# Where a convolution's layer norm and gate stand among the rounds of an attention

## The chip, the core and the metric

The kernel runs on one core of a Trainium2 chip. The metric is the device time of one execution in microseconds. Before the change it was 1478.38 us, the median of three runs (1476.76 to 1479.64).

## The reference

Two layers of a hybrid encoder, for 512 prompt tokens and 64 sample tokens (with a cache of 512). In each layer a normalised and modulated input goes through one projection. Half of its columns feed a sparse attention (8 heads, the best 256 or fewer keys per query). The other half feeds a convolution module, and both halves meet in one output projection:

```
g = a * jax.nn.sigmoid(b)
...
attn = dsa_attention(q, iq, iw, pos, k_all, v_all, ik_all, k_pos)
y = conv(padded) + conv_b                       # depthwise, width 31, 512 channels
y = jax.nn.silu(layer_norm(y, ln_conv_g, ln_conv_b))
mix = jnp.concatenate([attn, y], axis=-1)
x = x + gt_a * (mix @ w_out)
```

with `layer_norm(y) = (y - mean) * rsqrt(var + EPS) * g + b` over the 512 channels. A mixture of 16 experts follows in each layer.

## The kernel before

All tokens lie in five tiles: four of 128 (prompt) and one of 64 (sample). Channels lie on partitions for the convolution: `cy` is 128 x 4 x 576, four blocks of channels by all tokens. There is no planner; each engine has its own program written out by hand, and semaphores (`L["..."]`) tie them together. An engine works its list strictly in order.

The convolution is computed before the attention's softmax part. Its layer norm begins there as well: the mean is taken off `cy` on VectorE (L1461, `lnx`), the squares are made on GpSimd (L1785), summed over channels by TensorE with a matrix of ones (L720, L721), and scaled into `lnb`, the variance of every token, 128 x 576 (L1507, L1508, `lnr` = 1). What is left of it:

- the square root of `lnb` on ScalarE (L1162, `lnr` = 2)
- its reciprocal on VectorE (L1517)
- the product of `cy` with it on VectorE (L1519, `lny`)
- the gate function Silu on ScalarE, with the norm's gain and bias as the activation's scale and bias, one instruction for each of four channel blocks (L1178, `mixy`). It writes `hT[:, 4:8]`, half of the output projection's input.

The attention runs in ten rounds, n = 0 to 9, one for each group of four heads of one tile. The tiles come in the order 0, 4, 3, 2, 1, with 128, 576, 512, 384 and 256 keys. The stages of different groups overlap. In round n:

- TensorE turns group n's probabilities (L500 from L729), computes the logits of group n + 2 (L699, L700), in layer 0 also 16 matmuls of a later modulation in rounds 2 to 9 (L520), and multiplies group n's turned probabilities with V (L747).
- ScalarE copies the output of group n - 1 out (`outputs`, L1140), copies the turned probabilities of group n to SBUF (L1155), scales the probabilities of group n + 1 (`normalised`, L1132), and computes the exponentials of group n + 2 (`exps`, L1121).
- VectorE inverts the sums of group n + 1 (`inverses`, L1501), and adds the mask and takes the maxima of group n + 2 (`masked`, L1477, L1480, L1489).

In round 3 ScalarE's queue also issues the loads of gate vectors and norm vectors (L1168 to L1173), and in layer 0 in rounds 3 and 7 it stores modulation rows (`keep_mod`, L936).

Behind the rounds stands the output projection (`project_out`, L781): for each tile, 8 matmuls of 512 columns for each half of w_out. TensorE starts it once all four gate instructions (`mixy`) and all ten output copies (`on`) are there (L751, L752). The weights come through a ring of six slots; a slot is loaded by SyncE's queue (L378) when TensorE has released it.

ScalarE evaluates Exp, Sqrt and Silu from tables, and the program has an ACT_TABLE_LOAD where it goes from one to another. Copies and scalings have none of their own.

Of the kernel before, what the change touches and what calls it, by code (L numbers as in the profile page):

```python
# [20 lines left out]
ALU = mybir.AluOpType  # L21
ACT = mybir.ActivationFunctionType
AX = mybir.AxisListType

P = 128
# [5 lines left out]
TOK = SEQ + DEC  # L31
# [43 lines left out]
def rows_of(t):  # L75
    return P if t < 4 else DEC
# [23 lines left out]
def program(nc, A, O):  # L100
    ctx = ExitStack()
    with ctx:
        def sb(name, shape, dt=F32):
            return ctx.enter_context(nc.sbuf_tensor(name, shape, dt))

        def sem(name):
            return ctx.enter_context(nc.semaphore(name))
# [8 lines left out]
        hT = sb("hT", [P, KC, TOK])  # L116
# [3 lines left out]
        vT = sb("vT", [P, 52])  # L120
# [21 lines left out]
        def part(at, n, *shape):  # L142
            v = arena[:, at:at + n]
            if len(shape) == 2:
                return v.rearrange("p (a b) -> p a b", a=shape[0])
            if len(shape) == 3:
                return v.rearrange("p (a b c) -> p a b c", a=shape[0], b=shape[1])
            return v
# [8 lines left out]
        cy = part(17336, 2304, 4, TOK)  # L157
# [9 lines left out]
        lnb = part(8704, 576)  # L167
# [60 lines left out]
        L = {n: sem("l_" + n) for n in names}  # L228
# [61 lines left out]
        def chunks_of(t):  # L290

            return [(c, P) for c in range(t + 1 if t < 4 else 4)] + ([(4, DEC)] if t == 4 else [])
# [4 lines left out]
        def logit_bank(job):  # L297

            return job % 3 if job < 8 else job % 2 if job < 16 else (job + 2) % 3
# [605 lines left out]
        def _(act):  # L905
            S = nc.scalar
# [32 lines left out]
            for l in range(DEPTH):  # L939
# [13 lines left out]
                for k in range(0, KC, 2):  # L953
                    act.wait_ge(L["nT"], k + 1)
                    S.activation(hT[:, k, 0:SEQ], ps[k][:, :], ACT.Identity, bias=vT[:, k:k + 1],
                                 scale=small[:, S_AT + k:S_AT + k + 1]).then_inc(L["nTa"], 1)
                act.wait_ge(L["nT"], 9)
                for k in range(0, KC, 2):
                    S.activation(hT[:, k, SEQ:TOK], ps[0][:, k * DEC:(k + 1) * DEC], ACT.Identity, bias=vT[:, 16 + k:17 + k],
                                 scale=small[:, S_AT + 8 + k:S_AT + 9 + k]).then_inc(L["nTa"], 1)  # L960
# [152 lines left out]
                def exps(n):  # L1113
                    t, g = GROUPS[n]
                    m = rows_of(t)
                    act.wait_ge(L["nmx"], n + 1)
                    for i in range(4):
                        r = PR[0:m, 4 * (n % 2) + i, 0:NKEYS[t]]
                        h = S_SUM + 8 * ((n // 2) % 2) + 4 * g + i
                        q = S_NMX + 4 * (n % 2) + i  # L1120
                        ins = S.activation(r, r, ACT.Exp, bias=small[0:m, q:q + 1], accum_out=small[0:m, h:h + 1])  # L1121
                    ins.then_inc(L["pexp"], 1)

                def normalised(n):

                    t, g = GROUPS[n]
                    m = rows_of(t)
                    act.wait_ge(L["inv"], n + 1)
                    for i in range(4):
                        h = S_INV + 4 * (n % 2) + i  # L1130
                        r = PR[0:m, 4 * (n % 2) + i, 0:NKEYS[t]]
                        ins = S.mul(r, r, small[0:m, h:h + 1])  # L1132
                    ins.then_inc(L["pn"], 1)

                def outputs(n):

                    t, g = GROUPS[n]
                    m = rows_of(t)
                    act.wait_ge(L["pv"], n + 1)
                    S.copy(hT[:, g:g + 3:2, t * P:t * P + m],  # L1140
                           ps[6 + n % 2][:, 0:2 * m].rearrange("p (j t) -> p j t", j=2)).then_inc(L["on"], 1)
# [6 lines left out]
                for n, (t, g) in enumerate(GROUPS):  # L1148
                    m = rows_of(t)
                    if n >= 1:  # L1150
                        outputs(n - 1)
                    for q, (c, kn) in enumerate(chunks_of(t)):
                        job = PT0[n] + q
                        act.wait_ge(L["pt"], job + 1)
                        S.copy(pT[0:kn, c, 0:4 * m], ps[4 + job % 2][0:kn, 0:4 * m]).then_inc(L["pta"], 1)  # L1155
                    if n + 1 < len(GROUPS):
                        normalised(n + 1)
                    if n + 2 < len(GROUPS):
                        exps(n + 2)
                    if n == 7:  # L1160
                        act.wait_ge(L["lnr"], 1)
                        S.activation(lnb[:, :], lnb[:, :], ACT.Sqrt).then_inc(L["lnr"], 1)  # L1162
                    if n == 3:
                        act.wait_ge(L["lnr"], 1)
                        if l == 0:
                            act.wait_ge(s_mst, 64)
                            keep_mod(2)
                        act.dma_start(gt[:, 0, :], mrows[0, 2].broadcast_to([P, D])).then_inc(L["gt_ld"], 16)  # L1168
                        act.dma_start(gt[0:DEC, 1, :], mrows[1, 2].broadcast_to([DEC, D])).then_inc(L["gt_ld"], 16)
                        for b, q in enumerate((4, 3)):  # L1170
                            act.dma_start(AB[0][:, b, :], mrows[0, q].broadcast_to([P, D])).then_inc(L["ab_ld"], 16)
                            act.dma_start(AB[1][0:DEC, b, :], mrows[1, q].broadcast_to([DEC, D])).then_inc(L["ab_ld"], 16)
                        act.dma_start(gf[:, :], A["g_norm_ffn"][l:l + 1].broadcast_to([P, D])).then_inc(L["ab_ld"], 16)  # L1173
                    if l == 0 and n == 7:
                        keep_mod(3)
                act.wait_ge(L["lny"], 1)
                for c in range(4):
                    S.activation(hT[:, 4 + c, :], cy[:, c, :], ACT.Silu, bias=vT[:, 48 + c:49 + c],  # L1178
                                 scale=vT[:, 44 + c:45 + c]).then_inc(L["mixy"], 1)
                outputs(9)  # L1180
                if l == 0:
                    keep_mod(4)
# [102 lines left out]
        def _(dve):  # L1285
            V = nc.vector
# [22 lines left out]
            for l in range(DEPTH):  # L1309
                n_chain = [0]  # L1310

                def chain(ins):

                    n_chain[0] += 1
                    ins.then_inc(L["dch"], 1)
                    dve.wait_ge(L["dch"], n_chain[0])
# [147 lines left out]
                def masked(n):  # L1464

                    t, g = GROUPS[n]
                    m = rows_of(t)
                    mk = C[0:m, K_M0:K_M0 + P] if t == 0 else msk[0:m, MSK_AT[t]:MSK_AT[t] + NKEYS[t]]
                    if n >= 2:
                        dve.wait_ge(L["pt"], PT0[n - 2] + len(chunks_of(GROUPS[n - 2][0])))  # L1470
                    for i in range(4):
                        job = 4 * n + i
                        dve.wait_ge(L["lgt"], job + 1)
                        r = PR[0:m, 4 * (n % 2) + i, :]
                        k = min(NKEYS[t], 512)
                        mx = S_MX + i
                        ins = V.tensor_tensor_reduce(r[:, 0:k], ps[logit_bank(job)][0:m, 0:k], mk[:, 0:k], 0.125, MARK, ALU.add, ALU.max,  # L1477
                                                     small[0:m, mx:mx + 1])
                        if t == 4:
                            ins = V.tensor_tensor_reduce(r[:, 512:576], ps[2 + job % 2][0:m, 0:DEC], mk[:, 512:576], 0.125, MARK,  # L1480
                                                         ALU.add, ALU.max, small[0:m, mx + 4:mx + 5])
                        ins.then_inc(L["ttr"], 1)
                    dve.wait_ge(L["ttr"], 4 * n + 4)
                    if t == 4:
                        chain(V.tensor_tensor(small[0:m, S_MX:S_MX + 4], small[0:m, S_MX:S_MX + 4], small[0:m, S_MX + 4:S_MX + 8], ALU.max))
                    if n >= 2:
                        dve.wait_ge(L["pexp"], n - 1)
                    q = S_NMX + 4 * (n % 2)
                    V.tensor_scalar(small[0:m, q:q + 4], small[0:m, S_MX:S_MX + 4], -1.0, None, ALU.mult).then_inc(L["nmx"], 1)  # L1489
                    dve.wait_ge(L["nmx"], n + 1)  # L1490
# [18 lines left out]
                for n in range(len(GROUPS)):  # L1509
                    if n + 1 < len(GROUPS):  # L1510
                        inverses(n + 1)
                    if n + 2 < len(GROUPS):
                        masked(n + 2)
                    if l == 0 and n == 5:
                        add_bias(3, 3)
                dve.wait_ge(L["lnr"], 2)
                chain(V.reciprocal(lnb[:, :], lnb[:, :]))  # L1517
                dve.wait_ge(L["lnx"], 1)
                V.tensor_tensor(cy[:, :, :], cy[:, :, :], lnb[:, :].unsqueeze(1).to_broadcast([P, 4, TOK]), ALU.mult).then_inc(L["lny"], 1)  # L1519


                if l == 0:
# [331 lines left out]
```

## Time and profile before

| | |
|---|---|
| median of 3 runs | 1478.38 us |
| the profiled execution | 1482.77 us |
| its span, first to last instruction | 1480.9 us |
| mean granted TensorE clock | 0.896 |
| TensorE busy | 1252.0 us, 85% |
| VectorE busy | 551.3 us, 37% |
| ScalarE busy | 362.0 us, 24% |
| GpSimd busy | 152.5 us, 10% |

The ten rounds lie at about 334 to 418 us in layer 0 and 1065 to 1150 us in layer 1. Times in the rows are microseconds from the span's start. Idle time of an engine that is not the bottleneck costs nothing, so the table alone says little on a change within the rounds; the chain of waits and the timeline of the rounds do.

### The profile page before, as it was taken

What the parts mean: (1) busy time and instruction counts of PE and PEld (TensorE: products, weight loads), DVE (VectorE), ACT (ScalarE), POOL (GpSimd) and SP (SyncE); (2) the same over time, 40 slices, a digit from 0 to 9 for tenths busy, and PEclk for the clock granted to TensorE, in tenths of its full rate; (3) what the DMA queues carried; (4) which work ended last, traced back from release to release, by engine and by line L of the source; (5) the groups of instructions that cost most, each with busy time, mean ns of one, the idle gap of its engine ahead of it and who ended that gap; (6) DMA issues with size and microseconds to landing.
All of it is one profiled execution on the core that took longest, in us unless ns stands there. A gap on an engine that the chain in (4) does not pass through costs nothing.

```text
span 1480.9 us, 15896 instructions
## 1 busy us (share of the span) xinstructions
PE 1252.0 (85%) x6139; PEld 724.7 (49%) x6139; DVE 551.3 (37%) x1418; ACT 362.0 (24%) x828; POOL 152.5 (10%) x218
## 2 busy tenths in 40 slices
PE   3998799987899779999707998998777996999990
PEld 0552244443545466777504533454445454777770
DVE  1118687023244521111042058980324353311115
ACT  2124110036831111111122133001368111211111
POOL 0401140010001150000021013100100011000002
PEclk7999799987999889999857989899858997999995
DMA  9438996351941589999580120223211016699985
GB/s 363 121 114 318 359 310 184 105 198 57 308 170 56 191 285 346 365 366 368 189 288 4 57 69 29 72 54 105 66 49 30 0 58 234 205 364 370 361 300 210
DMA packets 137173, 284.97 MB, mean 192 GB/s; under 512 B 11613, under 2 KB 91909, under 8 KB 130697
## 3 DMA queue, kind: packets, MB, share of 16 engines
q1 hardware_dynamic: 116416, 209.70, 42.0%
q0 software_dynamic: 8352, 42.50, 8.4%
q10 hardware_dynamic: 12329, 31.74, 6.1%
q8 instruction: 49, 0.80, 0.2%
q14 instruction: 27, 0.22, 0.0%
HBM read 237.91 MB, written 52.40 MB: 196 GB/s over the span
## 4 chain that ended last, share of the span: by engine, by line
PE 70%; DVE 11%; DMA 6%; ACT 6%; issue 4%; SPq 1%; POOL 1%; ACTq 1%; DVEq 0%; POOLq 0%
PE ps L490 46%; PE ps L781 9%; PE ps L500 6%; PE ps L639 3%; PE ps L700 3%; ACT arena L1121 2%; DMA W<-in_w_gate 2%; DMA X<-in_x_sample 2%; DVE arena L1426 1%; SPq L400 1%; DMA arena<-y_d,sid 1%; DVE arena L1477 1%; PE ps L520 1%; PE ps L600 1%; DVE arena L1387 1%
## 5 line engine op out<-in xcount | busy, mean ns | idle before, releaser
L490 PE MATMUL ps<-W,arena 128*128 128x256 f32 (+1 forms) x1280 | 347.0, 427 | 8.5 <-DMA W<-in_w_gate 3.2
L490 PEld LDWEIGHTS ps<-W,arena 128*128 128x128 f32 x1280 | 241.8, 193 | 83.3 <-issue 53.6
L490 PE MATMUL ps<-W,hT 128*128 128x512 f32 (+3 forms) x480 | 190.6, 557 | 7.7 <-DVE gt L1305 7.7
L500 PE MATMUL ps<-C,arena 128*128 128x128 f32 (+3 forms) x851 | 127.3, 295 | 65.3 <-ACT arena L1155 15.7
L500 PEld LDWEIGHTS ps<-C,arena 128*128 128x128 f32 (+3 forms) x851 | 104.1, 157 | 102.3 <-issue 32.1
L781 PE MATMUL ps<-W,hT 128*128 128x512 f32 (+1 forms) x320 | 144.8, 607 | 5.7 <-ACT hT L1178 5.7
L490 PE MATMUL ps<-hT,W 128*128 128x64 f32 (+1 forms) x512 | 142.6, 440 | 7.1 <-ACT arena L1044 7.1
L490 PEld LDWEIGHTS ps<-W,hT 128*128 128x128 f32 (+1 forms) x480 | 86.9, 184 | 110.4 <-issue 87.2
L490 PEld LDWEIGHTS ps<-hT,W 128*128 128x128 f32 x512 | 78.9, 193 | 72.2 <-issue 64.3
L781 PEld LDWEIGHTS ps<-W,hT 128*128 128x128 f32 (+1 forms) x320 | 57.1, 183 | 80.1 <-issue 73.7
L1689 DVE TENSOR_TENSOR arena<-arena,ps 128x256 f32<-128x256 f32 x32 | 13.5, 421 | 215.1 <-ACT arena L1219 215.1
L1386 DVE MAX8 small<-arena 64x8 f32<-64x576 f32 (+3 forms) x132 | 80.5, 610 | 3.7
L1387 DVE MATCH_REPLACE8 arena<-small,arena 64x576 f32<-64x576 f32 (+3 forms) x132 | 78.4, 594 | 0.0
L639 PE MATMUL ps<-arena 128*32 128x64 f32 (+1 forms) x1024 | 66.5, 418 | 5.3 <-DMA arena<-arena 5.3
L1790 POOL DMA_INDIRECT x_d<-arena,sid x30 | 28.8, 960 | 380.1 <-DVE sid L1599 366.8
L520 PE MATMUL ps<-W,scT 128*32 128x512 f32 x384 | 58.3, 706 | 11.1 <-DMA W<-in_w_ada 10.7
L700 PE MATMUL ps<-arena 64*128 64x128 f32 (+4 forms) x160 | 56.2, 623 | 10.9 <-DVE small L1477 10.5
L1818 POOL DMA_INDIRECT arena<-y_d,sid x20 | 20.1, 1004 | 403.7 <-DMA y_d<-arena 200.3
L1219 ACT ACTIVATE arena<-ps 128x256 f32<-128x256 f32 x32 | 12.3, 383 | 190.8 <-PE ps L490 190.8
L1121 ACT ACTIVATE arena<-arena,small 128x128 f32<-128x128 f32 (+4 forms) x80 | 47.3, 592 | 44.4 <-DVE small L1489 44.3
L1684 DVE COPY arena<-ps 128x512 f32<-128x512 f32 x32 | 22.1, 691 | 93.1 <-PE ps L490 93.1
L1477 DVE CUSTOM_DVE_ANT_0 arena<-ps,arena 64x512 f32<-64x512 f32 (+3 forms) x64 | 35.9, 587 | 55.6 <-PE ps L700 55.1
(244 smaller groups left out, 1106.8 us busy)
## 6 DMA issues: line engine op xcount, KB each, us to landing
W<-in_w_ada SPq DMA_DIRECT2D x48, 1024.0 KB, 7.5
W<-in_w_gate SPq DMA_DIRECT2D x32, 1024.0 KB, 10.4
W<-in_w_up SPq DMA_DIRECT2D x32, 1024.0 KB, 12.8
W<-in_w_down SPq DMA_DIRECT2D x32, 1024.0 KB, 7.7
arena<-x_d SPq DMA_DIRECT2D x33, 512.0 KB, 11.1
y_d<-arena ACTq DMA_DIRECT2D x33, 512.0 KB, 7.3
W<-in_w_in SPq DMA_DIRECT2D x16, 1024.0 KB, 7.3
arena<-arena SPq DMA_DIRECT2D x128, 79.2 KB, 2.1
```

The lines of the kernel that those rows point to most:

```text
L490: ins = T.matmul(out, l, r, start=n == 0, stop=n == len(pairs) - 1, skip_group_check=True)
L500: count(T.transpose(o, i, ident[0:m, 0:m]), done if n == len(outs_ins) - 1 else None)
L520: ins = T.matmul(out[32 * j:32 * j + 32, :], scT[:, k, :], W[:, use % 6, 512 * j:512 * j + 512], start=k == 0, stop=k == KC - 1, skip_grou ...
L639: ins = T.matmul(ps[b][32 * g:32 * g + 32, 0:n], W4[:, i % 2, NQ * g + q, :], G4[i % 2][:, g, s0 + 4 * q:s0 + 4 * q + n], start=q == 0, st ...
L700: T.matmul(ps[logit_bank(job)][0:rows_of(t), 0:b - a], q, kT[1][hp, a:b], start=True, stop=True).then_inc(L["lgt"], 1)
L781: ins = T.matmul(ps[5 + n % 3][0:rows_of(t), :], hT[:, 4 * q + k, tokens(t)], wv[:, k, :], start=q == 0 and k == 0, stop=last, skip_group_ ...
L1121: ins = S.activation(r, r, ACT.Exp, bias=small[0:m, q:q + 1], accum_out=small[0:m, h:h + 1])
L1386: chain(V.max(m8, sc))
L1387: chain(V.match_replace(sc, m8, sc, MARK))
L1477: ins = V.tensor_tensor_reduce(r[:, 0:k], ps[logit_bank(job)][0:m, 0:k], mk[:, 0:k], 0.125, MARK, ALU.add, ALU.max, small[0:m, mx:mx + 1])
L1684: V.tensor_copy(ys[:, u, 512:1024], ps[7][:, :]).then_inc(L["yd"], 1)
L1790: G.indirect_dma_start(out=x_d[:, :], out_offset=bass.IndirectOffsetOnAxis(ap=table[0:m, 5 * k + t:5 * k + t + 1], axis=0), in_=HR[0:m, t, ...
```

## The change

The four leftover steps of the layer norm are moved into the rounds; none is added or taken away:

- the square root, on ScalarE, from round 7 to round 0 (behind the exponentials of group 2)
- the reciprocal, on VectorE, from behind round 9 to round 2 (behind the maxima of group 4)
- the product, on VectorE, from behind round 9 to round 3 (behind the maxima of group 5)
- the four gate instructions, on ScalarE, from behind round 9 to round 7 (behind the exponentials of group 9, where the square root was)

```
-                    if n == 7:
+                    if n == 0:
                         act.wait_ge(L["lnr"], 1)
                         S.activation(lnb[:, :], lnb[:, :], ACT.Sqrt).then_inc(L["lnr"], 1)
...
+                    if n == 7:
+                        act.wait_ge(L["lny"], 1)
+                        for c in range(4):
+                            S.activation(hT[:, 4 + c, :], cy[:, c, :], ACT.Silu, bias=vT[:, 48 + c:49 + c],
+                                         scale=vT[:, 44 + c:45 + c]).then_inc(L["mixy"], 1)
                     if l == 0 and n == 7:
                         keep_mod(3)
-                act.wait_ge(L["lny"], 1)
-                for c in range(4):
-                    S.activation(hT[:, 4 + c, :], cy[:, c, :], ACT.Silu, bias=vT[:, 48 + c:49 + c],
-                                 scale=vT[:, 44 + c:45 + c]).then_inc(L["mixy"], 1)
                 outputs(9)
...
                         masked(n + 2)
+                    if n == 2:
+                        dve.wait_ge(L["lnr"], 2)
+                        chain(V.reciprocal(lnb[:, :], lnb[:, :]))
+                    if n == 3:
+                        dve.wait_ge(L["lnx"], 1)
+                        V.tensor_tensor(cy[:, :, :], cy[:, :, :], lnb[:, :].unsqueeze(1).to_broadcast([P, 4, TOK]),
+                                        ALU.mult).then_inc(L["lny"], 1)
                     if l == 0 and n == 5:
                         add_bias(3, 3)
-                dve.wait_ge(L["lnr"], 2)
-                chain(V.reciprocal(lnb[:, :], lnb[:, :]))
-                dve.wait_ge(L["lnx"], 1)
-                V.tensor_tensor(cy[:, :, :], cy[:, :, :], lnb[:, :].unsqueeze(1).to_broadcast([P, 4, TOK]), ALU.mult).then_inc(L["lny"], 1)
```

## Rows read from the trace of the kernel before

**Rows 1.** The page, parts 1 and 4: busy engines, and the chain's shares.

```profile
PE 1252.0 (85%) x6139; PEld 724.7 (49%) x6139; DVE 551.3 (37%) x1418; ACT 362.0 (24%) x828; POOL 152.5 (10%) x218
...
PE 70%; DVE 11%; DMA 6%; ACT 6%; issue 4%; SPq 1%; POOL 1%; ACTq 1%; DVEq 0%; POOLq 0%
```

**Rows 2.** Chain of waits, layer 1's end: start, us, engine and line.

```profile
1137.28 1.28 ACT L1162
...
1145.15 1.28 ACT L1178
...
1146.45 3.15 ACT hT L1178 x4
...
1149.94 15.26 PE ps L781 x31
```

**Rows 3.** Chain of waits, layer 0's end.

```profile
408.56 3.77 DVE arena L1517
...
412.35 2.57 DVE arena L1519
...
414.95 0.87 ACT hT L1178
...
418.44 1.82 PE ps L781 x3
```

**Rows 4.** Timeline, layer 1's end: start, us, engine, line, count [idle before, released by].

```profile
1139.17 0.35 ACT L1140 COPY hT<-ps 128x256 f32<-128x256 f32 x1
...
1144.55 0.58 ACT L1155 COPY arena<-ps 128x512 f32<-128x512 f32 x1 [0.27 <-PE ps L500]
...
1145.28 1.97 PE L747 MATMUL ps<-arena,vrow 128*64 128x128 f32 x16 [0.77 <-ACT arena L1155]
...
1149.49 0.35 ACT L1140 COPY hT<-ps 128x256 f32<-128x256 f32 x1
```

**Rows 5.** Timeline, layer 0's end.

```profile
408.69 1.07 ACT L1155 COPY arena<-ps 128x512 f32<-128x512 f32 x2
...
409.91 1.09 PE L747 MATMUL ps<-arena,vrow 128*64 128x128 f32 x16
...
411.41 1.09 PE L500 MATMUL ps<-C,arena 128*128 128x128 f32 x8 [0.41 <-ACT arena L1132]
...
413.20 1.28 ACT L1178 ACT_TABLE_LOAD   x1
...
414.29 1.09 PE L747 MATMUL ps<-arena,vrow 128*64 128x128 f32 x16
```

**Rows 6.** Timeline, ScalarE in round 1, layer 1 and then layer 0.

```profile
1074.96 2.77 ACT L1132 ACTIVATE arena<-arena,small 64x576 f32<-64x576 f32 x4
...
1079.67 0.78 ACT L1121 ACTIVATE arena<-arena,small 64x576 f32<-64x576 f32 x1 [1.94 <-DVE small L1489]
...
348.87 0.78 ACT L1121 ACTIVATE arena<-arena,small 64x576 f32<-64x576 f32 x1 [1.94 <-DVE small L1489]
```

**Rows 7.** Timeline, layer 1, the small reciprocals of groups 4 and 5 and group 4's scaling.

```profile
1094.56 0.18 DVE L1501 RECIPROCAL small<-small 128x4 f32<-128x4 f32 x1 [3.05 <-ACT arena L1121]
...
1097.03 2.56 ACT L1132 ACTIVATE arena<-arena,small 128x512 f32<-128x512 f32 x4
...
1105.50 0.18 DVE L1501 RECIPROCAL small<-small 128x4 f32<-128x4 f32 x1 [3.05 <-ACT arena L1121]
```

**Rows 8.** Layer 0's end: SyncE's queue, and w_out's issues with time to landing.

```profile
405.62 6.52 SPq L378 DMA_DIRECT2D W<-in_w_out  x4
...
W<-in_w_out SPq DMA_DIRECT2D x4, 1024.0 KB, 7.1
```

**Rows 9.** Windows: us, busy by engine, granted clock (PEclk), DMA share, GB/s.

```profile
418.00:424.00 6.00, 5.56 (x9) 2.41 (x10) 0.00 (x0) 0.34 (x2) 0.00 (x0) 0.72 1.08 358
1137.00:1147.00 10.00, 5.59 (x40) 4.77 (x40) 6.49 (x3) 8.44 (x16) 0.00 (x0) 0.64 0.00 0
1149.00:1155.00 6.00, 5.06 (x8) 2.27 (x9) 0.00 (x0) 0.84 (x2) 0.00 (x0) 0.63 0.01 3
```

## The prediction

> **What bounds the kernel now.** I read the page's shares and its chain first. TensorE is busy for 85% of the span, but that is a mean over stages; the chain gives it 70%, with ScalarE and VectorE taking turns in between [rows 1]. The change touches only the ten attention rounds of each layer, so I read the chain of waits there, and then the timeline around each moved instruction. At the end of layer 1's rounds ScalarE alone carries the chain: table load and square root, copies, table load and the four gate activations, then the output projection at 1149.94 [rows 2]. At the end of layer 0 the chain goes through VectorE: square root, reciprocal 3.77 us, product 2.57 us, gate, projection at 418.44 [rows 3]. So the same code ends differently in the two layers, and each has to be summed for itself. Everything behind the projection hangs on its start, so I let a shift here pass on whole.
>
> **Edit 1, square root from round 7 to round 0.** In round 7 the table load of 1.28 and the square root stand ahead of the next copy: it starts at 1139.17, where without it it could have started at about 1137.18 (the exponentials are done at 1137.27, and a copy starts 0.1 ahead of that end), so 2.0 us [rows 2, 4]. In round 0 the same 2.0 us come behind the exponentials of group 2. Round 7 used no exponential after it; round 0 does, so a load for the exponential is added once per layer, 1.28 us, behind the scaling of group 2 and ahead of the exponentials of group 3. Loads need not wait for the data: the one for the gate in layer 0 ran at 413.20, and the gate then waited for the product that ended at 414.92 [rows 3, 5]. So I place it in the idle time if there is any. There is: the scaling runs from 1074.96 for 2.77 us, and the exponentials of group 3 wait 1.94 us for VectorE's maxima and start at 1079.67; layer 0 has the same 1.94 us [rows 6]. Nothing behind the maxima of group 3 needs what is delayed (its logits and maxima follow from scaled group 1). New start: 1079.73 (scaling done, 2.0 later) + 0.02 + 1.28 + 0.02 = 1081.05, so 1.38 us later than before. From there ScalarE's exponentials, its copies out of PSUM and TensorE's transposes alternate, and I see no second idle time on ScalarE that belongs to an outside event. I take +1.38 us in each layer. Bounds: 0, if a later round absorbs it (idle before exponentials exists in nearly every round, but is itself set by the loop), and 3.27 (2.0 + 1.28), if none of it is covered.
>
> **Edit 2, reciprocal and product into rounds 2 and 3 on VectorE.** Behind the maxima of group 4 VectorE sits idle for 3.05 us up to the small reciprocal of group 4 at 1094.56 [rows 7]. The wide reciprocal needs 3.77 there, so the small one comes 0.7 late, at about 1095.3; its reader, ScalarE's scaling, starts only at 1097.03 [rows 7], so 1.7 us are left: no cost. The product needs 2.57, and the idle time before the small reciprocal of group 5 (1105.50) is 3.05 again: no cost. If the cover were gone, each would cost its excess over 3.05, at most 0.7 us per layer. What it takes off is the chain of 3.77 and 2.57 at the end of layer 0, and nothing in layer 1, where ScalarE is late anyway. GpSimd issues nothing in these rounds, and no DMA is moved past either.
>
> **Edit 3, the gate from behind the rounds into round 7.** Load and four activations take 1.28 + 3.15; from the load to the next copy it is 1149.49 - 1145.15 = 4.34 us [rows 2, 4]. In round 7 it stands in the square root's place, ahead of the copy of group 7's output, the copies of group 8's transposes, its product with V, the transposes and copies of group 9. All of these move by 4.34 - 1.90 (load to copy before, 1139.17 - 1137.28 = 1.89) = +2.45 us, since ScalarE has no idle time there that it could use.
>
> *Layer 1's end.* Before: the last copy ended at 1145.13, TensorE's product of group 9 ran from 1145.28 for 1.97 us to 1147.25, quite hidden under the gate. After: it ends at 1147.25 + 2.45 = 1149.70; then the output copy that it releases (0.04 + 0.37), and 0.10 to the projection: 1150.21 against 1149.94 [rows 2, 4], +0.27 us. The gate leaves the end, and the product behind it comes into view.
>
> *Layer 0's end.* Before, VectorE's chain kept the projection to 418.44. After: transposes of group 9 at 411.41 + 2.45 = 413.86, 16 modulation matmuls behind them and the product of group 9, which began at 414.29, at 416.74; + 1.09 + 0.41 + 0.10 = 418.34 [rows 3, 5]: -0.10 us. The last w_out load waits for a slot that these transposes release: it is issued at 412.14 at the latest now, 414.6 then, and lands 7.1 us later at about 421.7 [rows 8]; it is needed by the thirteenth matmul of the projection, 418.34 + 12 x 0.43 = 423.5 [0.43: 13.3 of the chain's 15.26 us for 31 matmuls at full clock, rows 2]. Hidden, with 1.8 us to spare.
>
> Sum without the clock: layer 0 +1.38 - 0.10 = +1.28, layer 1 +1.38 + 0.27 = +1.65, together +2.93 us.
>
> **TensorE's clock.** In layer 0 it idled 3.06 us under the gate (product done at 415.38, projection at 418.44) and the projection's first 6 us were granted 0.72 of the clock: 6 x 0.28 = 1.7 us lost. In layer 1 the clock was at the low level, 1.2 GHz, already for the last product, and the projection's first 6 us got 0.63 [rows 4, 5, 9]: 2.2 us lost over these, 1.7 of it behind 1149.94. After the change the wait right before the projection is about 0.5 us in both. Against that a new wait of 2.3 us opens in layer 0 (the copies that the product of group 8 needs are over at 408.69 + 1.07 + 2.45 = 412.21, so it moves from 409.91 to 412.25 [rows 5], while the matmuls before it end where they did), and in layer 1 the wait in round 7 grows from 3.7 to 6.1 us with the clock already down behind it. Bounds: 3.4 us back (both projections at 2.4 GHz at once), or as much lost (a later rise in the longer pauses of rounds 1 to 3 in both). I take 0.7 us back, near the lower end, because the pause is moved and not removed.
>
> Forecast: +2.93 - 0.7 = +2.2 us. The profiled execution took 1482.77 us (span 1480.9 and 1.9 around it), so 1485.0 for such a one; it lies 4.4 above the median of the plain runs, 1478.38, so I predict 1480.6.
>
> *A rule that speaks against the change.* The trace shows 1.28 us for a load, with the gate 0.02 behind it [rows 2]. The Trainium skill ("ScalarE: Activation LUTs", "What ACT_TABLE_LOAD costs") adds a drain of about 1.38 us to each change of set. By it round 0's two loads would be 2.76 dearer, and the sum 5.5 us higher, 1486.1. The trace contradicts it: in layer 1's end the last copy is over at 1145.13 and the load begins at 1145.15 [rows 2, 4], so there is no room for a drain, and this rule gets no chance of its own. The page's other rule, all exponentials first and then all square roots, is what the kernel before obeys and this change breaks: by the trace's price that is the 1.28 us per layer of edit 1.
>
> **The rivals.**
> *The clock pays for it (chance 0.2).* The shift of 2.93 stands, but TensorE enters both projections at full clock: 2.93 - 3.4 = -0.5 us, 1477.9. For it: the wait right before them shrinks from 2.7 and 3.1 to 0.5 us. Against: rows 9 show the low clock well before layer 1's projection.
> *The shift is absorbed (0.1).* The reload hides in later rounds' idle time, +1.38 goes to 0 twice, and with the clock's 3.4 it is 0.17 - 3.4 = -3.2 us, 1475.2: faster. For it: ScalarE idles before most exponentials. Against: each such idle time is ended by VectorE's maxima, which follow from ScalarE's own earlier copies.
> *The pauses cost the clock more (0.2).* The longer pause in round 1 and the one in round 7 keep the clock low for longer, in each layer by as much as the pause before the projection costs now, 1.7: +2.93 + 2 x 1.7 = +6.3 us, 1484.7, slower. It decides if the rounds' matmuls behind the pause run at 1.2 GHz where they ran at 2.4 before. For it: layer 1's rounds 1 to 3 already run low. Against: the clock is low there anyway, so there is little to lose.
> The forecast itself, no change to slightly slower, has 0.5. That the work leaves the end but not the chain is the forecast's core, so a change that doesn't do what it says is no further case.
>
> **How the numbers follow.** About 0.2%, 3 us, is what a measurement here can tell from no change. The forecast's own range is +1 to +4 us, and a third of it lies above 3; with the 0.2 of the costly pauses that makes slower 0.4. Faster is 0.1, the absorbed shift; the rest, 0.5, is within 0.2%. The range leaves out most of the faster case and the far end of the slower: 1476.9 to 1484.2.
>
> **What would show it.** The round-0 step is right if a third table load sits between the scaling of group 2 and the exponentials of group 3, with these some 1.4 us later relative to the round's start. VectorE: small reciprocal of group 4 later, its scaling not. The end is right if no gate stands before the projection and TensorE's pause there is near 0.5 us, with pauses of 2.3 (layer 0) and 6.1 us (layer 1) ahead of the product of group 8. I am wrong if the time from the first maxima of the rounds to the projection shrinks in either layer, or if it grows by over 4 us.

## The result

The changed kernel takes 1483.58 us in the median of 19 runs (1478.26 to 1489.95), the kernel before 1478.35 us (1476.76 to 1480.97) in 19 runs beside it: a ratio of 1.0039, 95% interval [1.0027, 1.0051]. The change costs about 5 us. The forecast was 1480.6, and the time lies within its range of 1476.9 to 1484.2. The sign was right and so were the steps of the schedule. The clock's term was wrong in size and in sign, and the time lies in the range only because two of its errors offset each other.

### The profile page after: what moved, and what is told of

Its sections match the earlier page's. It is cut to its first block, busy times and chain, and to the rows that moved or that the text cites. A ratio compares the mean times of both kernels' runs of the same rounds, so it can differ in the third digit from the quotient of the medians.

```text
span 1481.7 us, 15900 instructions
## 1 busy us (share of the span) xinstructions
PE 1250.6 (84%) x6139; PEld 723.0 (49%) x6139; DVE 551.7 (37%) x1418; ACT 365.0 (25%) x830; POOL 152.4 (10%) x218
## 4 chain that ended last, share of the span: by engine, by line
PE 71%; DVE 10%; ACT 7%; DMA 5%; issue 4%; SPq 1%; POOL 1%; ACTq 1%; DVEq 0%; POOLq 0%
PE ps L490 47%; PE ps L781 8%; PE ps L500 6%; PE ps L639 3%; PE ps L700 2%; ACT arena L1121 2%; DMA X<-in_x_sample 2%; SPq L400 1%; PE ps L520 1%; DVE arena L1427 1%; DMA arena<-y_d,sid 1%; PE ps L600 1%; DMA W<-in_w_gate 1%; DVE arena L1388 1%; PE ps L747 1%
## 5 line engine op out<-in xcount | busy, mean ns | idle before, releaser
L490 PE MATMUL ps<-W,hT 128*128 128x512 f32 (+3 forms) x480 | 187.3, 549 | 6.3 <-DVE gt L1306 6.3
L781 PE MATMUL ps<-W,hT 128*128 128x512 f32 (+1 forms) x320 | 141.4, 595 | 1.0 <-issue 1.0
## 6 DMA issues: line engine op xcount, KB each, us to landing
W<-in_w_gate SPq DMA_DIRECT2D x32, 1024.0 KB, 10.4
```

The lines of the kernel that those rows point to most:

```text
L490: ins = T.matmul(out, l, r, start=n == 0, stop=n == len(pairs) - 1, skip_group_check=True)
L781: ins = T.matmul(ps[5 + n % 3][0:rows_of(t), :], hT[:, 4 * q + k, tokens(t)], wv[:, k, :], start=q == 0 and k == 0, stop=last, skip_group_ ...
```

## The profile after

The page of the changed kernel, parts 1 and 4, beside [rows 1]:

```profile
PE 1250.6 (84%) x6139; PEld 723.0 (49%) x6139; DVE 551.7 (37%) x1418; ACT 365.0 (25%) x830; POOL 152.4 (10%) x218
...
PE 71%; DVE 10%; ACT 7%; DMA 5%; issue 4%; SPq 1%; POOL 1%; ACTq 1%; DVEq 0%; POOLq 0%
```

ScalarE has two more instructions and 3.0 us more, of which the two added table loads are 2.6. Nothing else of the change can be seen on the page. The chain of waits of the changed kernel, layer 0, rounds 0 and 1 (start, us, engine and line), shows the loads in place:

```profile
342.41 1.28 ACT L1162
...
343.71 0.68 ACT arena L1162
344.39 0.26 ACT hT L1140
344.65 0.49 ACT arena L1155
345.14 2.66 ACT arena L1132 x4
347.80 0.02 issue
347.82 1.28 ACT L1121
349.10 0.01 issue
349.11 3.14 ACT arena L1121 x8
```

Root, copies, scaling, reload (the added table load that brings the exponential back) and exponentials stand without a gap: the idle 1.94 us of [rows 6] are filled, and what doesn't fit is on the path. From the start of the exponentials of group 2 to those of group 3 it was 8.49 us before, and is 9.86 in layer 0 and 9.85 in layer 1 now: +1.37 and +1.36.

VectorE's side in layer 1 (timeline of the changed kernel), beside [rows 7]:

```profile
1093.32 3.75 DVE L1517 RECIPROCAL arena<-arena 128x576 f32<-128x576 f32 x1
...
1097.10 0.18 DVE L1502 RECIPROCAL small<-small 128x4 f32<-128x4 f32 x1
1098.80 2.55 ACT L1132 ACTIVATE arena<-arena,small 128x512 f32<-128x512 f32 x4
```

The small reciprocal comes late and its reader doesn't: ScalarE's scaling starts 1.77 us later than before, exactly as late as the whole layer is at that point.

The end of layer 1 (timeline of the changed kernel), beside [rows 4]:

```profile
1139.33 1.28 ACT L1177 ACT_TABLE_LOAD   x1
...
1140.63 3.14 ACT L1177 ACTIVATE hT<-arena,vT 128x576 f32<-128x576 f32 x4
1143.67 0.35 ACT L1140 COPY hT<-ps 128x256 f32<-128x256 f32 x1
...
1145.13 1.98 PE L747 MATMUL ps<-arena,vrow 128*64 128x128 f32 x16 [6.11 <-ACT arena L1155]
...
1149.61 1.09 PE L747 MATMUL ps<-arena,vrow 128*64 128x128 f32 x16 [0.77 <-ACT arena L1155]
...
1151.21 4.96 PE L781 MATMUL ps<-W,hT 128*128 128x512 f32 x11 [0.51 <-issue]
```

From load to copy 4.34 us, the pause in round 7 6.11, the one before the projection 0.51. The last product took 1.97 us before and takes 1.09 now: TensorE is at 2.4 GHz again before the projection, where it rose only within it before.

The end of layer 0 (chain of the changed kernel), beside [rows 3, 5]:

```profile
411.81 1.28 ACT L1177
...
417.61 1.55 PE ps L747 x16
419.16 1.93 PE ps L500 x8
421.09 2.07 PE ps L520 x16
423.16 1.02 PE ps L747 x16
424.18 0.52 issue
424.70 7.53 PE ps L781 x17
```

Here TensorE paused for 2.40 us before 417.61, the new pause, and the clock was at 1.2 GHz behind it: transposes that took 1.09 us take 1.93, and the end is 1.1 us later than forecast. The windows of the changed kernel (columns as in [rows 9]) show the same, the fall ahead of the projection in layer 0 and full clock in both projections:

```profile
418.00:424.00 6.00, 6.00 (x54) 3.62 (x49) 0.69 (x1) 2.61 (x6) 0.00 (x0) 0.72 0.98 357
424.00:430.00 6.00, 5.48 (x17) 2.46 (x14) 0.00 (x0) 0.37 (x1) 0.00 (x0) 1.00 0.99 320
1151.00:1157.00 6.00, 5.79 (x14) 2.71 (x15) 0.00 (x0) 0.11 (x1) 0.00 (x0) 1.00 0.01 3
```

And one thing that the forecast's sum didn't have. From the exponentials of group 4 to those of group 7, rounds 2 to 5, layer 0 took 29.0 us before (360.74 to 389.78) and takes 34.1 (360.98 to 395.04). The windows over round 3 and behind it, first of the kernel before, then of the changed one:

```profile
374.00:399.00 25.00, 21.47 (x185) 12.07 (x186) 7.29 (x30) 20.11 (x49) 0.00 (x0) 1.00 1.00 351
```

```profile
374.00:399.00 25.00, 21.87 (x155) 12.10 (x152) 5.83 (x22) 15.58 (x38) 0.00 (x0) 0.80 0.92 301
```

TensorE is as busy and gets 30 matmuls less done. The fall comes in round 3's pause, in which ScalarE's sequencer issues seven loads. First the kernel before, then the changed one, TensorE's timeline:

```profile
376.60 1.15 PE L500 MATMUL ps<-C,arena 128*128 128x128 f32 x8 [2.60 <-ACT arena L1155]
```

```profile
377.82 1.97 PE L500 MATMUL ps<-C,arena 128*128 128x128 f32 x8 [2.73 <-ACT arena L1155]
...
379.72 4.06 PE L700 MATMUL ps<-arena 64*128 64x384 f32 x8
```

The pause is 0.13 us longer and ends 1.2 us later, 2.4 us later counted from the exponentials of group 2. Before, the clock held through it; after, it was at 1.2 GHz for 10.2 us (its record in the trace; the granted 0.80 of 25 us says the same). From group 5 to group 7 that costs 4.2 us (19.4 before, 23.6 now).

The other 0.8 of the 5.0 us are lost from group 4 to group 5 (9.6 before, 10.4 now), ahead of round 3's pause. TensorE's pause in round 1 grew from 2.92 to 3.86 us, and the stretch at 1.2 GHz around it lasts 2 us further into the rounds. The windows, first of the kernel before, then of the changed one:

```profile
361.00:364.00 3.00, 3.00 (x50) 1.55 (x44) 0.18 (x1) 2.67 (x8) 0.00 (x0) 0.91 0.25 38
```

```profile
361.00:364.00 3.00, 3.00 (x31) 0.69 (x20) 3.00 (x1) 2.91 (x8) 0.00 (x0) 0.59 0.00 0
```

The profiled spans themselves (1480.9 before, 1481.7 after) don't show the 5 us, since the profile of before was a long one: it ran 4.4 us above its median, and between the projection of layer 0 and the rounds of layer 1, with the same instructions in all kernels, it is 1 to 9 us longer than each other profile of this case (5.9 longer than the changed kernel's). So the balance is made of the steps that the change touches, read from one profile of each kernel: +1.37 twice, +5.0 in rounds 2 to 5 of layer 0, +1.0 at its end, -1.7 in its projection, +0.3 in round 4 of layer 1, -0.8 at its end, -1.7 in its projection: +4.8, against 5.2 between the medians.

## The experiments

The theory: the schedule is as forecast, and the rest is TensorE's clock; the layer comes 1.4 us later, and the pause of round 3 then takes the clock down. The rival: the moved instructions do it themselves, wherever they stand. The measure for both is one distance in layer 0, from the start of the exponentials of group 4 to that of group 7. Beside it stand TensorE's pause in round 3 and the granted clock from 374 to 399 us:

| kernel | shift of group 3's exponentials | pause in round 3 | clock, 374 to 399 | group 4 to 7 | median, us | before, beside it |
|---|---|---|---|---|---|---|
| before | 0 | 2.60 | 1.00 | 29.0 | 1478.35 | |
| changed | +1.37 | 2.73 | 0.80 | 34.1 | 1483.58 | 1478.35 |
| changed, again | +1.37 | 2.74 | 0.80 | 34.3 | 1482.52 | 1478.11 |
| e1_gate_behind | +1.38 | 2.80 | 0.80 | 34.2 | 1479.42 | 1478.11 |
| e2_root_before | 0.00 | 2.63 | 1.00 | 29.1 | 1475.16 | 1478.11 |
| e3_both | 0.00 | 2.62 | 1.00 | 29.0 | 1474.71 | 1478.11 |
| e3_again | 0.00 | 2.54 | 1.00 | 29.0 | 1473.78 | 1476.44 |
| f1_late | +0.53 | 2.76 | 0.86 | 31.7 | 1480.92, one run | 1477.05 |
| f3_late | +1.57 | 2.79 | 0.80 | 33.9 | 1484.19, one run | 1477.05 |
| f5_late | +2.61 | 2.62 | 1.00 | 29.5 | 1483.90, one run | 1477.05 |
| g_after_pool | +1.37 | 0.24 | 1.00 | 27.6 | 1476.45 | 1477.05 |
| g_root_gate_pool | 0.00 | 0.24 | 1.00 | 26.7 | 1468.74 | 1476.44 |

**The changed kernel again.**

> The changed kernel once more, for a second profiled execution. Theory A (schedule and clock): the exponentials of group 3 come 1.37 us late in each layer as in the first profile, but the place and length of the stretches at 1.2 GHz in layer 0's rounds 3 to 9 differ from the first profile, where one of 10.2 us began in round 3's pause; the median is 4 to 6 us above the kernel before, and single executions lie up to 11 us apart. Theory B (the changed instructions themselves are slow, or something behind the rounds): the same steps lose time in both profiles, 5 us in rounds 3 to 5 of layer 0, whatever the clock.

1.0031 [1.001, 1.0052] of the kernel before. The step to group 3 is +1.37 in layer 0 and +1.38 in layer 1; the stretch at 1.2 GHz in layer 0's round 3 is there again, 10.2 us long, and costs 5.3 us. I had expected it to lie elsewhere: it doesn't wander. The later stretches do differ a little (in layer 1's rounds it lasts 44.4 us in place of 37.5). Single runs are 11.5 us apart, as expected. Theory B's "in both profiles" came true as well, so this run alone didn't decide between the two.

**The gate back behind the rounds.**

```
 # e1: the changed kernel, with
-                    if n == 7:
-                        act.wait_ge(L["lny"], 1)
-                        ... four Silu ...
+                act.wait_ge(L["lny"], 1)
+                ... four Silu ...
                 outputs(9)
```

> Square root in round 0, reciprocal and product in rounds 2 and 3, but the gate behind round 9 as before. Theory A: each layer pays 1.38 us for the load back to the exponential, and round 7 is rid of load and root (1.9 us); layer 0 also of the wait for VectorE (0.5): 1.38 - 2.4 - 1.0 with rounding, layer 0 -1.0, layer 1 -0.6, so 1.6 us below the kernel before (1476.7), and 4.5 to 7 below the changed kernel. Rival (the pause in round 0 and 1 costs the clock, the gate in round 7 nothing): no better than the changed kernel, 3 to 5 us above the kernel before.

1.0015 [0.9995, 1.0036]: 3.1 us below the changed kernel, less than I had thought, and no gain on the kernel before. In the profile the two ends together gain 4.2 us where 4.4 were worked out, but not where they were: from the exponentials of group 9 to the projection -0.96 us in layer 0 and -3.21 in layer 1 against the kernel before (the changed kernel: +1.00 and -0.78), where -2.4 and -2.0 had been worked out. In layer 0 ScalarE, rid of the root, waits for TensorE instead (0.57 and 0.65 us ahead of its two output copies), whose modulation matmuls stand ahead of the products. So the gate in round 7 costs 2.0 and 2.4 us per layer against the same place behind the rounds. But layer 0 loses 5.2 us in rounds 2 to 5 here too: the gate has nothing to do with that.

**The square root ahead of round 0.**

```
 # e2: the changed kernel, with
                 normalised(0)
+                act.wait_ge(L["lnr"], 1)
+                S.activation(lnb[:, :], lnb[:, :], ACT.Sqrt).then_inc(L["lnr"], 1)
 ...
-                    if n == 0:
-                        ... the same two lines ...
```

> The changed kernel with the square root ahead of round 0, behind the scaling of group 0. Theory A: both table loads fall into ScalarE's idle times (5.0 us before the first copy, 3.6 before the exponentials of group 2), so the 1.38 us of each layer are gone, 2.8 below the changed kernel, and the exponentials of group 3 follow those of group 2 by 8.5 us again as in the kernel before. Rival (the gate in round 7 and its longer pause is what costs): less than 1 us below the changed kernel.

0.9987 [0.9969, 1.0005] of the kernel before, and 7.4 us below the changed kernel where I had said 2.8. Both loads are hidden, the root's and the one back to the exponential (ScalarE's timeline, layer 0):

```profile
330.26 1.28 ACT L1148 ACT_TABLE_LOAD   x1
334.87 0.68 ACT L1148 ACTIVATE arena<-arena 128x576 f32<-128x576 f32 x1 [3.33 <-DVE arena L1508]
...
337.37 1.28 ACT L1121 ACT_TABLE_LOAD   x1
340.95 0.77 ACT L1121 ACTIVATE arena<-arena,small 64x576 f32<-64x576 f32 x1 [2.30 <-DVE small L1489]
```

The exponentials of group 3 follow those of group 2 by 8.48 us, as before. The surplus of some 4.6 us is the clock's: the stretch in round 3 is gone, and group 4 to group 5 takes 9.6 us again. Its windows, with the same reciprocal, product and gate as the changed kernel:

```profile
374.00:399.00 25.00, 21.45 (x180) 11.80 (x179) 7.33 (x31) 19.54 (x47) 0.00 (x0) 1.00 1.01 351
```

**Both.**

```
 # e3: root ahead of round 0 (as e2), gate behind the rounds (as e1)
```

> The square root ahead of round 0, reciprocal and product in rounds 2 and 3, the gate behind round 9 as before. Theory A: nothing is added, and 1.9 us of round 7 in each layer and 0.5 of VectorE's chain in layer 0 are taken off: 4.4 us below the kernel before, 1474.0. Rival (it is late in layer 0 on something else, or the clock takes it back): within 1.5 us of the kernel before.

> The same kernel with the loads on ScalarE's queue, once more, for the comparison on one chip and for a second profile: 3 to 4 us below the kernel before, layer 0's rounds 3 to 8 at 2.4 GHz.

0.9977 [0.9957, 0.9997] and, on another chip, 0.9975 [0.9961, 0.9989]: 3.4 and 2.7 us below the kernel before, where 4.4 were worked out. It keeps what the change is good for, VectorE's work off layer 0's end and the root out of round 7, and its one added table load a layer lies in idle time. The missing microsecond or more is at layer 0's end, which gained 0.96 us here too and not 2.4.

**A delay without the change.** The kernel before, with k copies whose result nobody reads:

```
                     act.wait_ge(L["nmx"], n + 1)
+                    if n == 3:                              # ahead of group 3's exponentials
+                        act.wait_ge(L["lnr"], 1)
+                        for j in range(k):                  # k = 1, 3, 5
+                            S.activation(fill[:, j, :], C[:, 0:512], ACT.Copy)
```

> The kernel before with one added copy of 512 columns on ScalarE (about 0.5 us) ahead of the exponentials of group 3, whose result nothing reads; nothing of the change in it. Theory A (layer 0 loses 5 us in rounds 3 to 5 because everything there comes later, so that the pause of round 3 takes TensorE's clock down): a shift this small may or may not do it; between exponentials of group 4 and group 7 either 29.0 us as before or up to 34. Rival B (the change's own instructions do it): 29.0 us.

> The kernel before with three such copies (about 1.4 us) ahead of the exponentials of group 3, as late as the reload makes them in the changed kernel. Theory A: from the exponentials of group 4 to those of group 7 layer 0 takes 34 us in place of 29.0, with a stretch at 1.2 GHz that begins at the pause of round 3. Rival B (the change's own instructions, the root or the wide reciprocal on VectorE, do it): 29.0 us, and TensorE stays at 2.4 GHz through rounds 3 to 8.

> The kernel before with five such copies (about 2.3 us) ahead of the exponentials of group 3. Theory A in its plain form (any delay does it): 34 us again. Theory A' (it depends on where the pause comes to lie, so the loss is no growing function of the delay): back toward 29 to 31 us. Rival B: 29.0 us.

With three copies (+1.57 us) the loss is there in full, 4.9 us, with none of the change in the kernel: the rival falls. With five copies, a longer delay, it is gone but for 0.4. With one it is 2.6, with the clock at 0.86. So most of what is lost in these rounds, 4.2 of the 5 us, is not for the delay itself, but for the clock that falls in round 3's pause. (With five copies the 0.4 us stand ahead of that pause, from group 4 to group 5.) The delay has its own price beside that: the three whole times, one run each, are 1480.92, 1484.19 and 1483.90, so five copies made the kernel no faster than three. From group 2's exponentials to the projection the three lose 3.1, 6.4 and 3.0 us in layer 0 and 0.7, 1.3 and 2.2 in layer 1 against the kernel before. The windows and TensorE's row behind round 3's pause, with three copies:

```profile
374.00:399.00 25.00, 21.61 (x152) 11.86 (x151) 5.83 (x22) 15.59 (x37) 0.00 (x0) 0.80 0.96 305
```

```profile
377.51 1.97 PE L501 MATMUL ps<-C,arena 128*128 128x128 f32 x8 [2.79 <-ACT arena L1160]
```

and with five:

```profile
374.00:399.00 25.00, 21.45 (x193) 12.82 (x196) 7.30 (x31) 19.38 (x46) 0.00 (x0) 1.00 1.00 348
```

```profile
378.53 1.15 PE L501 MATMUL ps<-C,arena 128*128 128x128 f32 x8 [2.62 <-ACT arena L1160]
```

These are one profile each.

One rival is left by the table: that the pause's length decides. Every pause of 2.54 to 2.63 us in round 3 held the clock, and every one of 2.73 to 2.80 lost it. Among them is f1_late's, 2.76 us long, which ends only 0.3 us later than that of the kernel before, counted from group 2's exponentials; so the length may well have its part. The same profiles refute it as a general rule. Ahead of layer 0's projection the kernel before and f5_late pause equally long. First the kernel before, whose projection was granted 0.72 of the clock [rows 9], then f5_late with its window:

```profile
418.44 1.82 PE L781 MATMUL ps<-W,hT 128*128 128x512 f32 x3 [3.06 <-ACT hT L1178]
```

```profile
420.37 10.11 PE L782 MATMUL ps<-W,hT 128*128 128x512 f32 x23 [3.06 <-ACT hT L1183]
```

```profile
420.00:426.00 6.00, 5.63 (x13) 2.58 (x14) 0.00 (x0) 0.27 (x2) 0.00 (x0) 1.00 1.08 358
```

And a pause of 2.40 us lost the clock in the changed kernel (before 417.61), while e3_both's projection behind one of 2.61 was granted 1.00. So length alone doesn't tell which pause loses the clock; for round 3's pause no run holds its length and moves only its place.

**The pause taken away, the shift kept.** The changed kernel with round 3's loads on another queue (with semaphores of their own, counted over both layers):

```
 # ScalarE, round 3
-                        act.dma_start(gt[:, 0, :], ...)     # and six more
 # GpSimd, ahead of its scatters
+                pool.wait_ge(L["lnr"], 1)
+                pool.wait_ge(L["pexp"], 6)
+                if l == 0:
+                    pool.wait_ge(s_mst, 64)
+                pool.dma_start(gt[:, 0, :], ...)            # and six more
```

> The changed kernel, with the seven loads of gate and norm vectors issued from GpSimd's queue (behind the exponentials of group 5) and no longer from ScalarE's in round 3. This takes most of round 3's pause away. Theory A: the clock stays up through rounds 3 to 8 of layer 0, the 5 us are gone, and some 2 us per layer of the pause itself: 7 to 9 us below the changed kernel. Rival B (the loss has another cause than the pause): only the 2 us per layer, 4 below the changed kernel, and the exponentials of group 7 in layer 0 come over 3 us too late still.

1.0 [0.9986, 1.0013] of the kernel before: all that the change cost is paid back, 4.6 to 5.8 us by the ratios to the kernel before beside each; I had said 7 to 9. In the profile rounds 2 to 5 of layer 0 take 27.6 us, 6.5 less than the changed kernel's, though group 3 is late by the same 1.37 us, and TensorE's row behind the former pause reads:

```profile
376.15 1.14 PE L501 MATMUL ps<-C,arena 128*128 128x128 f32 x8 [0.24 <-ACT arena L1156]
```

Its windows:

```profile
374.00:399.00 25.00, 23.83 (x222) 14.06 (x222) 8.30 (x33) 21.64 (x54) 3.83 (x7) 1.00 1.00 315
```

The seven issues are now GpSimd's 3.83 us, beside everything else. In layer 1 the step from group 5 to group 6 falls by 3.3 us against the kernel before. Part of that is lost again behind it: from group 6 to the projection layer 1 takes 1.8 us more than in the changed kernel, and TensorE has 0.58 of the clock from 1141 to 1147, at the projection's start.

**The best of all.** e3 with the loads on GpSimd's queue:

> Root ahead of round 0, reciprocal and product in rounds 2 and 3, gate behind round 9, and the seven loads on GpSimd's queue. Theory A: the gains add: round 3's pause goes in both layers (2.3 us each and, in layer 1, some time at 2.4 GHz more), so 3 to 6 us below the same kernel with the loads on ScalarE's queue and 6 to 9 below the kernel before. Rival: with the gate behind round 9 something else ends last (the vectors' arrival for the projection's epilogue, or the clock falls elsewhere), and it is within 2 us of the same kernel with the loads on ScalarE's queue.

0.995 [0.9931, 0.9969]: 7.7 us below the kernel before and 5.0 below e3 on the same chip, as worked out. This version is faster than both kernels.

## Why the forecast was right, and where it wasn't

- *Edit 1, +1.38 us a layer:* measured +1.37 and +1.36, again +1.37 and +1.38. e2 takes it away by using the idle time that ScalarE has ahead of round 0. The rival that a later round absorbs it is refuted: it holds to the rounds' end in layer 1 (+1.36 at group 3, 1.64 at group 9).
- *Edit 2, no cost:* right. The small reciprocal is late (1097.10), and its reader starts 1.7 us after its start, as worked out.
- *Edit 3:* the pauses came as forecast: 2.40 us in layer 0 (2.3), 6.11 in layer 1 (6.1), 0.5 before the projection. +0.27 in layer 1 was -0.78: the last product ran at 2.4 GHz already and took 0.88 us less. -0.10 in layer 0 was +1.00: there the clock fell behind the new pause, and the transposes alone took 0.84 us more. Most of both differences is thus the clock's.
- *The clock, -0.7 us, is the step that failed.* At the ends it gave back more than I took: 3.4 us in the two projections and 1.05 at layer 1's end, less 1.1 at layer 0's, so -3.35. What I left out is +5.0 us in rounds 2 to 5 of layer 0 (and 0.3 in layer 1). The term came to +2.0 in place of -0.7. I had priced the pauses of rounds 1 to 3 by what a pause before the projection costs, 1.7 us, gave it to both layers, and said that the clock was low there anyway. That is so in layer 1, and in layer 0 only until 361; round 3's pause, at full clock and with 16 modulation matmuls in each round behind it, was the place to look at. The costly-pause rival had the right condition (matmuls behind a pause at 1.2 GHz where they ran at 2.4 before), but at a wrong place. It named the longer pauses of rounds 1 and 7. Round 1's did keep the clock low for longer in layer 0, and that cost 0.8 us; 4.2 are lost at round 3's, which is 0.13 us longer and comes 2.4 us later in the rounds. Its total of +6.3 against +5.2 is near by luck, since it left out the 3.4 us that the projections gave back.
- *Luck in the total:* with the 5.3 us of the rounds and without the 3.4 of the projections, the time would have been about 1487, outside the range. That it lies inside, 0.6 us from the upper bound, comes from two errors of opposite sign in the one term and not from the forecast's account of the clock.
- *The drain of the Trainium skill ("ScalarE: Activation LUTs", "What ACT_TABLE_LOAD costs"):* the reload in round 1 begins 0.02 us behind the scaling, and the exponentials 0.01 behind it. No drain is seen, as [rows 2, 4] had it. The price that the forecast gave this rule was too high as well: the root's load is moved and only one load a layer is added, so the rule would give 2.8 us more (an estimate from the 1.38 us of the section just named), and not 5.5. The batching rule of the Trainium skill ("ScalarE: Activation LUTs", "Table sets: the hidden batching unit"), all exponentials and then all square roots, bore out in the changed kernel: root and two loads are 3.3 us of work in rounds 0 and 1, of which 1.9 were hidden and 1.37 came on the path. But e2 and e3 break the rule just as much, with the same added load, and pay nothing for it.

What stays open: why single runs of the changed kernel are 12 us apart where those of the kernel before are 4 us apart in the first series (8 to 14 in the later ones), and what tells, to the microsecond, a pause that the clock survives from one that it doesn't; the length of the pause alone doesn't.

## What to carry to other kernels

Moving work off the end of a loop into its rounds paid here only where the engine that does it waits for something outside the ring of engines that hand to each other. In the ring, what was put in beyond ScalarE's idle time, 1.37 us, was still late at the rounds' end: the work left the end only to come back in the middle. Look for the idle time first (here ahead of round 0, 5 us wide), and count the table loads that the new order adds. And before pricing a shift at its own length, look at each pause of TensorE behind it that the clock has just survived. Taking the seven issues out of that pause was worth 5.0 us, more than the best placing of the four steps (2.7 to 3.4).

## What the runs showed of the hardware

- A shift of 1.4 to 1.6 us cost 5 us in the rounds behind it, beyond its own length, and one of 2.6 us cost 0.4, by whether TensorE's clock held through round 3's pause. This comes again in each profile of the same schedule: with the pause in place, four of four profiles with no shift held the clock, and four of four with a shift of 1.4 to 1.6 us lost it.
- The length of a pause alone didn't tell whether the clock fell: 3.06 us ahead of the projection held it in f5_late (1.00 granted) and lost it in the kernel before (0.72), and 2.40 us lost it in the changed kernel.
- Table loads didn't wait for the data of the activation behind them: in e2 the load at 330.26 was over 3.33 us before its square root could start. Both loads of a layer lay in such idle time and cost nothing (8.48 us between the exponentials of groups 2 and 3, as before).
- Seven DMA issues on ScalarE's queue, in layer 0 behind two stores, held its next copy back by 2.5 us in the kernel before and 2.65 in the changed one. On GpSimd's queue they took 3.83 us, and TensorE's pause shrank from 2.73 to 0.24 us.
